# Two of four down pairs as seven half products: a two-layer hybrid trunk on one core of Trainium2

## What is computed

```python
x = x + 0.5 * swiglu(rms_norm(x, ffn1_norm[l]), ffn1_w1[l], ffn1_w3[l], ffn1_w2[l])
...
x = x + merged @ w_out[l]
x = x + 0.5 * swiglu(rms_norm(x, ffn2_norm[l]), ffn2_w1[l], ffn2_w3[l], ffn2_w2[l])
```

## Time and profile before

| what | value |
|---|---|
| time, median of 3 runs | 2751.05 us (2750.5 to 2751.71) |
| profiled execution: its span, first to last instruction | 2748.1 us |
| TensorE busy in it | 2743.3 us |
| VectorE, ScalarE, GpSimd busy | 1851.7, 1335.1, 940.7 us |
| granted TensorE clock | 1.00 |
| mean DMA rate | 104 GB/s |

### The profile page before, as it was taken

The page is one execution under the profiler, slowest core; times in us unless marked ns, Lnnn a source line. Parts: engine busy times, 40 slices in busy tenths (PEclk is TensorE's granted clock), DMA queues, the critical chain, the costliest instruction groups (busy, mean ns, idle before and its releaser), DMA issues.

```text
span 2748.1 us, 41845 instructions
## 1 busy us (share of the span) xinstructions
PE 2743.3 (100%) x16054; PEld 2337.2 (85%) x16054; DVE 1851.7 (67%) x2984; ACT 1335.1 (49%) x2103; POOL 940.7 (34%) x466
## 2 busy tenths in 40 slices
PE   9999999999999999999999999999999999999999
PEld 8898888777788889898998988887777888898988
DVE  7686857885667448585785878578846674585755
ACT  6353444655355346353563534446553653553533
POOL 0135824433343442131121357244333434421221
DMA  5333583222222232233332335832222222322332
GB/s 171 108 108 116 151 180 107 84 71 72 83 85 85 85 100 94 92 116 100 108 108 92 116 115 159 171 108 84 70 73 81 86 83 85 100 99 94 108 98 102
DMA packets 113110, 284.80 MB, mean 104 GB/s; under 512 B 35617, under 2 KB 45345, under 8 KB 112417
## 3 DMA queue, kind: packets, MB, share of 16 engines
q1 hardware_dynamic: 112928, 282.35, 34.6%
HBM read 268.67 MB, written 9.44 MB: 101 GB/s over the span
## 4 chain that ended last, share of the span: by engine, by line
PE 99%; DVE 1%; ACT 0%; issue 0%; DVEq 0%; ACTq 0%
PE bank L627 22%; PE bank L629 22%; PE bank L628 22%; PE bank L676 7%; PE bank L677 7%; PE bank L678 7%; PE bank L653 1%; PE bank L655 1%; PE bank L654 1%; PE bank L1048 1%; PE bank L1067 1%; PE bank L1082 1%; PE bank L817 1%; PE bank L1181 1%; PE bank L1035 0%; PE bank L1240 0%
## 5 line engine op out<-in xcount | busy, mean ns | idle before, releaser
L476 POOL TENSOR_TENSOR w_lo<-raw,w_hi 128x1024 fp32r<-128x1024 f32 x208 | 519.8, 2504 | 872.1 <-ACT w_hi L468 872.1
L627 PE MATMUL bank<-h_hi,w_hi 128*128 128x512 f32 x1504 | 593.4, 395 | 0.5 <-DVE silu_a L2363 0.3
L629 PE MATMUL bank<-h_hi,w_lo 128*128 128x512 f32 x1504 | 585.8, 390 | 0.0
L628 PE MATMUL bank<-h_lo,w_hi 128*128 128x512 f32 x1504 | 585.8, 390 | 0.0
L468 ACT ACTIVATE w_hi<-raw 128x1024 fp32r<-128x1024 f32 x310 | 326.5, 1056 | 353.8 <-PE bank L629 313.5
L541 POOL TENSOR_TENSOR w_lo<-raw,w_hi 128x1024 fp32r<-128x1024 f32 x122 | 223.4, 1854 | 802.3 <-DVE bank L2308 802.3
L627 PEld LDWEIGHTS bank<-h_hi,w_hi 128*128 128x128 f32 x1504 | 282.3, 188 | 65.6 <-issue 7.1
L629 PEld LDWEIGHTS bank<-h_hi,w_lo 128*128 128x128 f32 x1504 | 282.4, 188 | 59.8
L628 PEld LDWEIGHTS bank<-h_lo,w_hi 128*128 128x128 f32 x1504 | 282.5, 188 | 56.4
L627 PE MATMUL bank<-g_hi,w_hi 128*128 128x512 f32 x698 | 271.9, 390 | 0.0
L628 PE MATMUL bank<-g_lo,w_hi 128*128 128x512 f32 x698 | 271.7, 389 | 0.0
(11 more groups left out here) (452 smaller groups left out, 5895.7 us busy)
## 6 DMA issues: line engine op xcount, KB each, us to landing
raw<-in_w_lots SPq DMA_DIRECT2D x478, 512.0 KB, 3.7
s_wd<-s_z SPq DMA_DIRECT2D x8, 512.0 KB, 2.7
s_t<-s_taps SPq DMA_DIRECT2D x16, 256.0 KB, 12.9
da_s<-da_qk SPq DMA_DIRECT2D x16, 256.0 KB, 4.1
x<-in_x SPq DMA_DIRECT2D x8, 256.0 KB, 5.5
raw_k<-in_w_lots SPq DMA_DIRECT2D x8, 256.0 KB, 5.6
s_w_im<-s_wd SPq DMA_DIRECT2D x32, 64.0 KB, 3.9
s_w_re<-s_wd SPq DMA_DIRECT2D x32, 64.0 KB, 2.5
```

The lines of the kernel that those rows point to most:

```text
L476: eng.tensor_tensor(w_lo[:, s], raw[:, s], w_hi[:, s].bitcast(f32), SUB).then_inc(S["lo_done"], 1)
L627: pe.matmul(b[:, :], w_hi[:, s, kw], xh[:, k], start=(k == 0), stop=False)
L628: pe.matmul(b[:, :], w_hi[:, s, kw], xl[:, k], start=False, stop=False)
L629: return pe.matmul(b[:, :], w_lo[:, s, kw], xh[:, k], start=False, stop=(k == nk - 1))
```

## The change

In the second FFNs, thirds 0 and 1 of both layers (`DOWN_HALVED`), the eight down lots are no longer all plain. Four (two pairs, `DOWN_LEAD`) stay plain, the first two of them side by side with k in the order 0, 4, 1, 5, 2, 6, 3, 7; the other two pairs are made in seven half products with sums of g. g is now kept whole in `g_whole`; VectorE makes the four sums of g block by block in the last up iterations, and the low parts of g late (`sums_of_g`, `lows_of_g`), where each g had its low part one iteration behind. S1 and S2 are rounded behind the last g, S3 and S4 once the four plain lots are done, since their rounded halves lie in quarters of g_hi and g_lo that only plain lots read. The constant `hgreset`, whose place some sums take, is loaded again in layer 0. In outline, with helpers passed by (the products q1 to q7 now take their operands from an object, `Up` or `Down`; `whole` on VectorE is renamed `pair_of_plain`; a semaphore is renamed; GpSimd's clearing of semaphores waits for a rounded g and not for its low part), and in the order of the constants, TensorE, SyncE, GpSimd, ScalarE, VectorE:

```diff
+DOWN_HALVED = ((), (0, 1))
+DOWN_ORDER = (0, 4, 1, 5, 2, 6, 3, 7)
+DOWN_LEAD = 2
...
+            def down_halved(which, th, n, g0):
+                for j in range(2):
+                    begin(n + j, 0, OUT[n + j])
+                for i, k in enumerate(DOWN_ORDER):
+                    pe.wait_ge(S["g_done"], g0 - KT + i + 1)
+                    for j in range(2):
+                        m = passes(bank[OUT[n + j] % 4], slot(n + j), k, g_hi, g_lo, k, KT)
+                        if k == KT - 1:
+                            m.then_inc(S["out_done"], 1)
+                for j in range(2, 2 * DOWN_LEAD):
+                    gemm(n + j, 0, g_hi, g_lo, KT)
+                halved(n + 2 * DOWN_LEAD, n + KT, Down(which, th))
...
-                    down(n, J, g0)
+                    down_halved(1, th, n, g0)
...
+                    if n == FIRST_LOT[1][2] + 8 and layer < DEPTH - 1:
+                        reset = CON_AT["hgreset"]
+                        sp.wait_ge(S["out_done"], OUT[FIRST_LOT[1][2]])
+                        sp.dma_start(con[:, reset:reset + SEQ], con_in[:, reset:reset + SEQ]).then_inc(S["c_rest"], 16)
...
+            def lows_of_pair(n, early=False):
+                if early:
+                    low_of(pool, n)
+                pool.wait_ge(S["x7_in_t_sum"], t_at(n, T3))
+                if not early:
+                    low_of(pool, n)
+                low_of(pool, n + 1, 4)
...
+                    if th in DOWN_HALVED[which]:
+                        n = FIRST_LOT[which][th] + 2 * J
+                        pool.wait_ge(S["lo_done"], LOT(n + 2 * DOWN_LEAD))
+                        for i in range(DOWN_LEAD, KT // 2):
+                            lows_of_pair(n + 2 * i, early=i == DOWN_LEAD + 1)
...
+            def round_gs(which, th, j, g0):
+                act.wait_ge(S["x4_in_g_sum"], 2 * LOADED + gs_at(which, th, 3))
+                if j in (S1, S2):
+                    act.wait_ge(S["gated_done"], g0)
+                else:
+                    act.wait_ge(S["out_done"], OUT[FIRST_LOT[which][th] + 2 * KT + 2 * DOWN_LEAD])
+                for k in range(4):
+                    ins = act.activation(gs_hi[j][:, k], gs_sum[j][k], AFT.Copy)
+                ins.then_inc(S["x6_in_g_hi"], 1)
+            def down_halved(which, th, n, g0):
+                d = n + 2 * DOWN_LEAD
+                round_gs(which, th, S1, g0)
+                round_gs(which, th, S2, g0)
+                high(act, d)
+                round_t(d, T1)
+                round_t(d, T3)
+                high(act, d + 1, 4)
+                round_t(d, T2)
+                round_t(d, T4)
+                high(act, d + 2)
+                round_gs(which, th, S3, g0)
+                copy_x(d)
+                round_gs(which, th, S4, g0)
+                for a in range(d, n + KT, 2):
+                    if a > d:
+                        high(act, a + 2)
+                        copy_x(a)
+                    round_weights(a + 2, a)
...
+            def sums_of_g(which, th, k, g):
+                V.wait_ge(S["gated_done"], g + k + 4 + 1)
+                one, two = slice(0, HALF), slice(HALF, SEQ)
+                a11, a12, a21, a22 = g_whole[:, k, one], g_whole[:, k + 4, one], g_whole[:, k, two], g_whole[:, k + 4, two]
+                s1 = do(TT(gs_sum[S1][k], a21, a22, SUB))
+                do(TT(gs_sum[S3][k], a11, a21, SUB))
+                need(s1)
+                chain(TT(gs_sum[S2][k], gs_sum[S1][k], a11, SUB))
+                TT(gs_sum[S4][k], a12, gs_sum[S2][k], ADD).then_inc(S["x4_in_g_sum"], 1)
+            def low_gs(which, th, j):
+                V.wait_ge(S["x6_in_g_hi"], 2 * LOADED + gs_at(which, th, GS_ORDER.index(j)))
+                for k in range(4):
+                    ins = TT(gs_lo[j][k], gs_sum[j][k], gs_hi[j][:, k].bitcast(f32), SUB)
+                ins.then_inc(S["c_ones_g_lo"], 1)
+            def down_halved(which, th, n):
+                d = n + 2 * DOWN_LEAD
+                for j in range(2, 2 * DOWN_LEAD):
+                    low_of(V, n + j)
+                low_gs(which, th, S1)
+                low_gs(which, th, S2)
+                for j in range(2 * DOWN_LEAD - 2):
+                    down(n, j, 0)
+                weights_t(d)
+                for j in range(2 * DOWN_LEAD - 2, 2 * DOWN_LEAD):
+                    down(n, j, 0)
+                low_gs(which, th, S3)
+                low_gs(which, th, S4)
+                for a in range(d, n + KT, 2):
+                    i = a - n
+                    if a > d:
+                        down_v(a - 2, i - 2)
+                        down_w(a - 2, i - 2)
+                    add_t(a + 2, T1)
+                    add_t(a + 2, T3)
+                    if a == d:
+                        take_y(a, 0)
+                    low_t(a + 2, T1)
+                    if a > d:
+                        down_y(a - 2, i - 2)
+                    add_t(a + 2, T2)
+                    low_t(a + 2, T3)
+                    low_t(a + 2, T2)
+                    add_t(a + 2, T4)
+                    if a > d:
+                        take_y(a, 0)
+                        down_x(a - 2, i - 2)
+                    low_t(a + 2, T4)
+                    second_of_v(i)
+                down_v(a, i)
+                down_w(a, i)
+                down_y(a, i)
+                down_x(a, i)
```

More of the change, by code:

```diff
@@ new lines, in blocks_of, with ready, __init__ @@
+            def blocks_of(whole, k0, cols):
+                return [whole[:, k0 + k, cols] for k in range(4)]
+            one, two = slice(0, HALF), slice(HALF, SEQ)
+            class Up:
+                x11, x12, x22 = ([blocks_of(a, k0, cols) for a in (h_hi, h_lo)] for k0, cols in ((0, one), (4, one), (4, two)))
+                sums = [[blocks_of(a[j], 0, one) for a in (s_hi, s_lo)] for j in range(4)]
+                def ready(self, j):
+                    pass
+            class Down:
+                x11, x12, x22 = ([blocks_of(a, k0, cols) for a in (g_hi, g_lo)] for k0, cols in ((0, one), (4, one), (4, two)))
+                sums = [[[gs_hi[j][:, k] for k in range(4)], gs_lo[j]] for j in S_SUMS]
+                def __init__(self, which, th):
+                    self.which, self.th = which, th
+                def ready(self, j):
+                    pe.wait_ge(S["c_ones_g_lo"], LOADED + gs_at(self.which, self.th, GS_ORDER.index(j)))
@@ L717, in q7, with halved @@
+            def q7(n, x):
                 pe.wait_ge(S["x5_in_yv"], y_at(n))
-                with_sums(x_bank(n), n, T3, S3).then_inc(S["x1_in_prod"], 1)
-            def halved(n, i0, J):
-                first = n + 2 * i0
-                for a in range(first, n + 2 * J, 2):
-                    q1(a)
+                x.ready(S3)
+                with_sums(x_bank(n), n, T3, x.sums[S3]).then_inc(S["x1_in_prod"], 1)
+            def halved(first, to, x):
+                for a in range(first, to, 2):
+                    q1(a, x)
@@ L1650, in three_plain @@
             def three_plain(n, g, which):
+                whole = 0 in DOWN_HALVED[which]
                 high_sum(2 * which)
@@ L1689, in six_plain, with halved @@
                 silu(n + 10, 1, g)
-            def halved(n, i0, J, g0):
+            def halved(n, i0, J, g0, whole=False):
                 for i in range(i0, J):
@@ L2393, in _, with down_v, down_w, down_y @@
             done = [0, 0]
+            def down_v(n, i):
+                V.wait_ge(S["x1_in_prod"], product_at(n, 7))
+                need(done_v[0])
+                STT(x[:, i + 1, HALF:SEQ], x_bank(n), -0.5, x[:, i + 1, HALF:SEQ], MUL, ADD).then_inc(S["x5_in_yv"], 1)
+            def down_w(n, i):
+                STT(x[:, i, 0:HALF], w_bank(n), 0.5, x[:, i, 0:HALF], MUL, ADD).then_inc(S["free%d" % (OUT[n] % 4)], 1)
+            def down_y(n, i):
+                V.wait_ge(S["out_done"], OUT[n] + 1)
+                done[0] = done[1] = do(STT(x[:, i + 1, 0:HALF], Y_BANK, 0.5, x[:, i + 1, 0:HALF], MUL, ADD))
@@ L2446, in six_plain, with halved @@
                 low_g(4, g)
-                whole(n + 10, 5)
+                pair_of_plain(n + 10, 5)
                 multiply(5, g)
-            def halved(n, i0, J, g0):
+            def halved(n, i0, J, g0, th=None):
+                whole = th is not None
                 for i in range(i0, J):
@@ L2457, in halved @@
                             need(done[i % 2])
-                            multiply(i - 2, g0)
+                            multiply(i - 2, g0, whole)
                         take_w(a - 2, i - 1)
@@ L2487, in halved @@
                         low_of(V, a + 3)
+                    if whole and i - 2 >= KT // 2:
+                        sums_of_g(1, th, i - 2 - KT // 2, g0)
+                        if more:
+                            lows_of_g(th, i - 2 - KT // 2, g0)
                 a = n + 2 * J - 2
```

195 lines of the change are left out of this document (117 added, 78 removed).

## The result

The changed kernel takes 2756.16 us (median, 2755.75 to 2756.78) against 2749.96 for the one before in the same comparison: a ratio of 1.0022, with a 95% interval of 1.0014 to 1.0030. It is 6.2 us slower. The forecast was 2755.8, in a range of 2746 to 2763, with 0.37 on slower by more than 0.2% and 0.53 on no change that shows; the result lies just past the bound of 0.2%, on the side that was given the smaller chance. The profiled execution spans 2754.5 us, 6.4 more than the 2748.1 of before.

A forecast was written before the change was run, and what follows sets the result against it. TensorE's product order bounds the kernel, other engines only where products wait. Four places lose 5.8 us, third 0's holes give back 1.1: +4.7, so span 2752.8; with the median's 2.95 above the span, 2755.8 us, range 2746 to 2763.

The forecast's parts named there:

- one queue order in the first halved down pair: VectorE's lows of S3 and S4 precede the T1 sum; q7 waits 2.2 us (D: the down part's first half product).
- ScalarE's short rounding without a row of its own: 256-column rounding from SBUF to SBUF, taken as 0.31 us to the next, bounded by 0.28 and 0.40.
- The plain part of the down stage: From first down product to the halved pairs, 21.8 us: g's late sums and lows stay hidden, no TensorE hole.
- the three signs that were to show the prediction wrong: Copy_v(d) by D+5.2, the plain part waiting for g's lows, or the granted clock leaving 1.00.
- the computed case: The summed forecast of 2755.8 us, bounded by 2753.5 to 2758 through ScalarE's rounding and some ten links; chance 0.55.
- Third 0's holes: Four TensorE holes behind third 0's halved up pairs go as low_g(2) leaves the queue before the T3 sum: 1.1 us less.
- rival (c): TensorE's clock falls behind the new 2.2 us standstills, adding 5.7 to 11.5 us: 2761.5 to 2767; chance 0.08.
- The second hole: Second halved down pair: 10.9 us from take_y to take_y on VectorE, so q7 is 0.7 us late.
- Rival (a): The sums are hidden: VectorE reaches the T3 sum by D+3.0, both waits go, 8.0 us gained: 2743; chance 0.10.
- Rival (b): A GpSimd low delays one VectorE low of S3 by about 1.2 us in each place: 2760.6; chance 0.12.
- Rival (d): Another late link, such as g's last low, costs 1 to 2 us a place: 2760 to 2764; chance 0.08.
- The 1.7 us of cover: Plain down part: slack before TensorE asks for g's late lows, forecast as hidden with 1.7 us to spare.

The follow-up runs named there:

- the eighth run: Kernel before, with VectorE's low_g(2) moved behind the subtraction take_y in the first halved pair of third 0; 2749.69 us, ratio 1.0001.
- the eleventh: Kernel after, both take_y subtractions and V's copy moved up, T4's sum and low part moved behind down_v in the second halved down pair; 2742.55 us, ratio 0.9973.
- the ninth run: Kernel after, with only ScalarE's copy of V in the first halved down pair moved ahead of the first two weight sums' roundings; 2748.75 us, ratio 0.9995.
- the third run: Kernel after, with both halved down pairs' take_y subtractions moved up on VectorE and the first pair's V copy on ScalarE; 2748.90 us, ratio 0.9996.
- the seventh: Kernel after, without VectorE's eight low-part instructions of S3 and S4 per place, TensorE multiplying the high parts instead; 2750.93 us, ratio 1.0004.
- tenth runs: Kernel after with both take_y subtractions and V's copy moved up, and without the low parts of S3 and S4; 2749.30 us, ratio 0.9996.

## Why the prediction was right, and where it was off

**The mechanism and the place held.** The largest risk taken was to put most of the loss on one queue order in the first halved down pair. Its links came as worked out: S3's lows at D+1.6, the T1 sum at D+4.6, the copy at D+7.0, take_y at D+7.4, q7 at D+7.9. Moving the copy alone gave 7.4 us back. The bound for ScalarE's short rounding without a row of its own is settled: four take 1.34 us, 0.31 from one to the next, the value taken. The plain part of the down stage has no hole either, as forecast: the low parts of g and the two lots' lows all fit under the 21.8 us. One of the three signs that were to show the prediction wrong did come, though: the granted clock left 1.00, to 0.96 in two places. This was given 0.08.

**The time was met partly by luck.** The forecast set +4.7 us on a median of 2751.05, of three runs; in the comparison before takes 2749.96. Set on that, it would be 2754.7, and 1.5 us too low. The two errors, 1.1 too high in the base and 1.5 too low in the change, nearly cancel in the 2755.8. Nor do the bounds of the computed case follow from their own terms: ten links by 0.05 us are 2.0 us in four places, so 2753.2 to 2759.2 and not 2753.5 to 2758.

**The sum, term by term.** The forecast was 4 x 1.45 - 1.1 = +4.7 us. The four places came out at 181.29 against 4 x 43.55 = 174.20, so +7.1; third 0's four holes are gone in both layers, -1.1; the remaining 0.4 of the 6.4 us between the two profiled spans is there before the first down part of layer 0 (its first product is at 94.16 against 93.68), in code that the change leaves alone, and goes with the wait at the start. Of the 1.3 us by which +5.8 was too small, two parts can be told:
- *The clock, rival (c), +0.8.* It was given 0.08, as a case apart at 5.7 us or more. It came in part: in two of four places, for some 0.4 us each. The slow products themselves cost more, but while they run VectorE catches up, and the second hole vanishes from these places; the loss and the hole behind it don't add here, since one chain sets both.
- *The second hole, +0.2 to 0.3 where the clock holds.* It is 0.98 us instead of 0.7: the chain from take_y to take_y took 11.10 us (2517.44 to 2528.54), not 10.9. Half of that is made up for by the rest, so that the places of layer 1 are 45.10 and 45.15 against 45.0: 0.13 a place, 0.5 in all.

**Third 0's holes: right size, reason shown in part.** I had them go because low_g(2) leaves the queue ahead of the T3 sum. In the eighth run it did, and the first pair's hole went. It stood behind the first subtraction instead, and the second pair's hole grew by what was won. In the kernel after no low_g stands in these pairs at all. Its trace has 10.31 us from the first subtraction to the second (1071.73 to 1082.04), the eighth run's 11.19 (1070.67 to 1081.86). That leaving it out is what removes the second hole is argued from these two traces, not shown by a run of its own.

**The rivals.** Rival (a), hidden sums at 2743, was no property of the work but of its order: the last version lands there, 2742.6. Its condition, the T3 sum by D+3.0, was not needed, though. In the ninth run the T3 sum stands at D+5.2 as in the kernel after, and 1.6 of the first 2.15 us are gone; in the eleventh it stands at D+5.55 and no wait is left. What counted was the copy that waited behind the roundings which the sums release. The prediction saw the copy in the chain and took its place behind the sum for given. Rival (b), GpSimd in VectorE's way, did not happen: the four lows of S3 take 1.43 us in all four places, like those of S4 and as worked out. In the place above GpSimd's low before them ends at D+0.3, where the prediction had D+0.2, and S3's lows begin at D+1.6. Rival (d), another late link, is not in the kernel after, but it is what the third run met as soon as the first two waits were gone. The 1.7 us of cover that (d) gives g's last low are those of g2 and g6; by the prediction's own times the last low ends at U+7.2 and is asked for at U+9.5, 2.3 us later. In the changed trace it ends at U+7.2 in layer 0's third 0 (U = 1117.24).

**After the prediction.** My expectation of the two subtractions together (2742.5) overlooked down_v. In the seventh and tenth runs I took an amount of work for the bound, where an order was; the idle times in front of VectorE's instructions, with their releasers, told that in each trace at once.

## What to carry to other kernels

When a wait ends at a chain that crosses engines, look at each instruction of it for what it needs and what it merely stands behind: here a 0.4 us copy stood behind two roundings of sums and half a lot's rounding, none of which it uses, on an engine that is half idle, and moving it was worth more than leaving out 2.9 us of VectorE's work. Before cutting TensorE's products, measure the other engine's chain between two products that wait for it against TensorE's work between them (here 11.1 against 10.0 us). Repair it one wait at a time and read the trace again: here the next link came up after 7.3 of the 13.6 us. A hole filled with other TensorE work did not help while the chain remained.

## What the runs showed of the hardware

TensorE's clock fell behind a standstill of 2 us, but not each time. TensorE's timeline in a layer 0 place of the kernel after, where the clock comes back, and the busy times from q7 on:

```profile
1150.92 0.41 PE L702 MATMUL bank<-g_hi,w_hi 128*128 128x256 f32 x1
1151.13 0.32 PE L703 MATMUL bank<-g_lo,w_hi 128*128 128x256 f32 x1
1151.29 0.28 PE L704 MATMUL bank<-g_hi,w_lo 128*128 128x256 f32 x1
```
```profile
1146.94:1149.00 2.06, 2.06 (x13) 2.06 (x13) 1.95 (x4) 0.60 (x1) 0.57 (x1) 0.71 0.00 0
1149.00:1151.00 2.00, 2.00 (x11) 2.00 (x11) 1.34 (x3) 0.79 (x2) 0.00 (x0) 0.50 0.00 0
1151.00:1153.00 2.00, 2.00 (x18) 2.00 (x18) 1.90 (x5) 1.02 (x2) 0.00 (x0) 0.95 0.89 238
```

The products start 0.21 us apart at a granted clock of 0.50 (1.2 GHz) and 0.12 apart at 1.00 (2.4 GHz). The fall begins up to 1.5 us behind the first product after the hole (1.0 us behind it in the place above, once at the very next product), and the slow products last 3.0 to 3.4 us. In the three profiled runs that have the hole of 2.15 us at all four places it came in 8 of 12 places, in a set that changed from one execution to the next (two, three and three of four); in the nine profiled runs of other versions, whose longest hole in such a place is between 0 and 1.6 us, in none of 36. What decides between the 8 and the 4, all behind a hole of 2.15 us, no run here shows. The Trainium skill, "TensorE: Matmul & The Clock Gate", section "Loop structure matters more than you think", has a TensorE that waits long between its matmuls fall to the lower clock; 8 of 12 places with a wait of 2 us agree with that here and 4 don't. The price was small, about 0.4 us net each, because the chain on VectorE went on meanwhile.
